# A projection with more rounded parts and one more tap for ScalarE and GpSimd, in a two-layer convolution and MLP trunk

## The reference

```python
u = rmsnorm(h, norm_mix[i])
a = jnp.einsum("bsd,de->bse", u, w_pw1) + b_pw1          # 2048 -> 4096
val, gate = jnp.split(a, 2, axis=-1)
v = val * jax.nn.sigmoid(gate)
v = causal_depthwise_conv(v, w_dw) + b_dw                # 31 taps, per channel
v = rmsnorm(v, g_norm)
v = jax.nn.silu(v)
return jnp.einsum("bsd,de->bse", v, w_pw2) + b_pw2       # "pw2"; then h = h + m
```

## Time and profile before

| | |
|---|---|
| median of 3 runs | 2257.8 us |
| the profiled execution's own time | 2257.75 us |
| its span, first to last instruction | 2256.0 us |
| PE / DVE / ACT / POOL busy | 99% / 63% / 51% / 7% of the span |
| the projection's stage | about 34 us to 215 us |
| mean granted clock of TensorE | 0.999 |

### The profile page before, as it was taken

One profiled execution on the slowest core, in us unless ns is written; L12 is line 12 of the kernel. 1 busy time (PEld: TensorE's weight loads), 2 busy tenths in 40 slices (PEclk: granted clock), 3 DMA queues, 4 the chain that ended last, 5 costly groups with the idle time before them and its releaser, 6 DMA issues.

```text
span 2256.0 us, 29803 instructions
## 1 busy us (share of the span) xinstructions
PE 2236.2 (99%) x10300; PEld 1864.8 (83%) x10300; DVE 1429.1 (63%) x1597; ACT 1145.3 (51%) x1424; POOL 157.1 (7%) x183
## 2 busy tenths in 40 slices
PE   8999999999999999999999999999999999999998
PEld 7998788888888888888888888888888888888886
DVE  6999776555545545566766667665456455556665
ACT  5666555535534534556644444555345345345555
POOL 3888000000000000000000000000000000000000
PEclk9999999999999999999999999999999999999999
DMA  9544477756756856777777677777567567567773
GB/s 340 166 155 145 145 251 256 236 193 206 255 190 196 269 187 204 251 222 256 221 241 220 217 241 213 264 231 253 189 196 267 191 202 252 199 215 224 261 241 112
DMA packets 494098, 494.86 MB, mean 219 GB/s; under 512 B 257936, under 2 KB 296016, under 8 KB 493264
## 3 DMA queue, kind: packets, MB, share of 16 engines
q1 hardware_dynamic: 492192, 491.31, 67.8%
q10 hardware_dynamic: 1696, 1.67, 0.2%
q0 software_dynamic: 144, 1.05, 0.1%
HBM read 460.42 MB, written 33.55 MB: 219 GB/s over the span
## 4 chain that ended last, share of the span: by engine, by line
PE 98%; DMA 1%; DVE 0%; ACTq 0%; issue 0%; ACT 0%; SPq 0%; DVEq 0%
PE acc L430 29%; PE acc L431 29%; PE acc L432 29%; PE acc L492 3%; PE acc L501 2%; PE acc L503 2%; PE acc L502 2%; PE acc L536 1%; PE acc L566 0%; PE acc L565 0%; PE acc L564 0%; DMA emb<-in_cf_b_pw 0%; ACTq L708 0%; DMA staged<-prows 0%; DMA pT<-staged 0%
## 5 line engine op out<-in xcount | busy, mean ns | idle before, releaser
L927 DVE TENSOR_TENSOR wlo<-raw,whi 128x1024 fp32r<-128x1024 f32 x728 | 880.6, 1221 | 590.1 <-ACT whi L586 586.3
L586 ACT ACTIVATE whi<-raw 128x1024 fp32r<-128x1024 f32 x728 | 762.2, 1057 | 774.8 <-PE acc L432 773.8
L430 PE MATMUL acc<-whi,b_hi 128*128 128x512 f32 x1632 | 635.5, 389 | 0.3 <-DVE b_lo L1028 0.3
L432 PE MATMUL acc<-whi,b_lo 128*128 128x512 f32 x1632 | 634.9, 389 | 0.0
L431 PE MATMUL acc<-wlo,b_hi 128*128 128x512 f32 x1632 | 634.9, 389 | 0.0
L430 PE MATMUL acc<-whi,a_hi 128*128 128x512 f32 x1280 | 497.9, 389 | 0.0
L432 PE MATMUL acc<-whi,a_lo 128*128 128x512 f32 x1280 | 497.9, 389 | 0.0
L431 PE MATMUL acc<-wlo,a_hi 128*128 128x512 f32 x1280 | 497.9, 389 | 0.0
L430 PEld LDWEIGHTS acc<-whi,b_hi 128*128 128x128 f32 x1632 | 306.3, 188 | 64.8 <-DVE b_lo L1028 0.7
L432 PEld LDWEIGHTS acc<-whi,b_lo 128*128 128x128 f32 x1632 | 306.3, 188 | 63.8
L431 PEld LDWEIGHTS acc<-wlo,b_hi 128*128 128x128 f32 x1632 | 306.3, 188 | 63.5 <-issue 0.2
(11 more groups left out here) (161 smaller groups left out, 1244.5 us busy)
## 6 DMA issues: line engine op xcount, KB each, us to landing
raw<-in_mlp_w SPq DMA_DIRECT2D x256, 1024.0 KB, 5.5
raw<-in_sc_w_in SPq DMA_DIRECT2D x48, 1024.0 KB, 5.7
raw<-in_cf_w_pw SPq DMA_DIRECT2D x64, 512.0 KB, 8.7
raw<-in_ple_w_gate SPq DMA_DIRECT2D x32, 1024.0 KB, 6.1
staged<-prows SPq DMA_DIRECT2D x240, 128.0 KB, 3.3
pT<-staged SPq DMA_DIRECT2D x56, 512.0 KB, 3.3
raw<-in_cf_w_pw SPq DMA_DIRECT2D x16, 1024.0 KB, 6.8
raw<-in_sc_w_out SPq DMA_DIRECT2D x16, 1024.0 KB, 7.6
```

Source lines behind the costliest of these rows:

```text
L430: nc.tensor.matmul(o, xhi[:, k, s], hi, start=first and c == 0, stop=False)
L432: mm = nc.tensor.matmul(o, xlo[:, k, s], hi, start=False, stop=last and c == 1)
L586: nc.scalar.activation(whi[:, e % SLOTS, :, :], raw[:, e // 2, 2 * (e % 2):2 * (e % 2) + 2, :], ACT.Copy).then_inc(hi_ready, 1)
L927: nc.vector.tensor_tensor(wlo[:, e % SLOTS, :, :], raw[:, e // 2, 2 * (e % 2):2 * (e % 2) + 2, :], whi[:, e % SLOTS, :, :].bitcast(F32), A ...
```

## The change

- `FULL` goes from 5 to 3: from chunk 1 on, 13 of the 16 parts are rounded. The pieces of x are parts 3 to 8 and 9 to 15.
- `POOL_TAPS` goes from 9 to 10: one more product on ScalarE and one more addition on GpSimd, one tap fewer on VectorE. VectorE's places for `front_w_lo` move one tap later with it; that of `glu(n+1)` stays.
- The rounded x (`front_x_hi`) lies where the residual h does. x is fetched a second time into h, in four transfers of SyncE after the last value half, between the first and the second quarter of pw2's weights. VectorE waits for them ahead of pw2's first bias addition.
- `front_w` alone now lies in the place of the embeddings, and the filler `front_end` goes.

```diff
-    FULL = KC - 11
-    X_PARTS = ((FULL, 10), (10, KC))
+    FULL = KC - 13
+    X_PARTS = ((FULL, 9), (9, KC))
     LAST_ORDER = (0, 4, 5, 1, 2, 6, 7, 3)
-    POOL_TAPS = 9
+    POOL_TAPS = 10
...
+        with ExitStack() as before_h:
+            front_x_hi = before_h.enter_context(nc.sbuf_tensor("front_x_hi", [P, KC - FULL, 2 * P], F32R))
         h = sb("h", [P, 2, D])
...
             front_w = before_emb.enter_context(nc.sbuf_tensor("front_w", [P, 2, 2, KC - FULL, P], F32R))
-            front_x_hi = before_emb.enter_context(nc.sbuf_tensor("front_x_hi", [P, KC - FULL, 2 * P], F32R))
         front_x_lo = X[0][0][:, FULL:, :]
         emb = sb("emb", [P, DEPTH, 2, D])
-        sb("front_end", [P, 256])
...
+        x_again = sem("x_again")
...
-            load_unit(pw2, t_in["cf_w_pw2"][0], None)
+            w_pw2 = t_in["cf_w_pw2"][0]
+            load(pw2.b, w_pw2, 0)
+            sp.wait_ge(val_done, CHUNKS)
+            for j in range(BLOCKS):
+                nc.sync.dma_start(h[:, :, j * NB:(j + 1) * NB], xtok(j)).then_inc(x_again, 16)
+            load(pw2.b + 1, w_pw2, NB)
+            with sp.Fori(2, BLOCKS) as j:
+                load(pw2.b + j, w_pw2, j * NB, 0, exchange(Result(pw2, j - 2)))
             load_mlp(0, pw2)
...
                     dve.wait_ge(bias2_early, 16)
+                    dve.wait_ge(x_again, 16 * BLOCKS)
                     b = bias2_first
```

## The result

The changed kernel takes 2273.49 us (median of four runs, 2272.96 to 2274.13) against 2257.78: ratio 1.0068, interval 1.0056 to 1.0081. It is slower by 15.7 us, three times what I forecast and outside my range. The profiled execution takes 2273.25, its span is 2271.5. Executions of the kernel before fall into two groups about 1.6 us apart (2257.4 to 2258.0, and 2259.0 to 2259.5), and those of most other versions spread likewise, so medians of few runs waver by that.

What follows compares the result with a forecast made beforehand. TensorE was taken as the bound before the change, the chain through VectorE, ScalarE and GpSimd after it. +3.9 us for the stage and +1.1 behind the last chunk, added to 2257.75, gave 2262.7 us; range 2256 to 2268.

Steps and rivals of the forecast that it cites:

- What bounds it: First projection: TensorE sets the pace at 12.21 us a chunk; a chain through VectorE, GpSimd and ScalarE is second, about 11.5.
- TensorE's saving: First projection: fewer full and more rounded products save TensorE 0.146 us a half, 0.29 a chunk, giving a pace of 11.92.
- the split sizes: Rounded blocks grow from 1408 to 1664 columns: VectorE's split takes 1.88 us (+0.26), ScalarE's rounding 1.58 (+0.22).
- the head: Start of the projection: VectorE's two splits of x grow by 0.52 us, moving the first gated product from 34.01 to 34.53.
- The chain up to split B: Within a chunk, additions, products and rounding delay VectorE's gate-half weight split (split B) to +9.84 us from the gated product.
- product 9's wait: ScalarE's last tap product waits 0.18 us for a buffer that GpSimd's second single addition frees, starting at +7.83.
- The rival in which it doesn't wait: ScalarE's last tap product finds its buffer free: period 12.25 us, total 2260.2 us; chance 0.18.
- The step that failed: End of a chunk: VectorE's gate-half split starts unhindered at +9.84 us, two taps follow, next gated product at +12.43.
- this rival: GpSimd's sixth addition holds VectorE's gate-half split 0.72 us, 14 times: +10, 2272.8 us; half the chunks, 2267.7; chance 0.17.
- Behind the last chunk: After the projection's last chunk, GpSimd's late join delays ScalarE's copy and the norm, and TensorE's embedding products: +1.1 us.
- The fetch: Second fetch of x: four 512 KB transfers land by about 230 us, 35 us before their first reader; no cost.
- The later stages are untouched: Stages after the projection and embedding products: the change was taken to add no time there.

Runs made afterwards that it cites:

- v1: Changed kernel with ScalarE's rounding for the gate-half weight split moved into its wait for GpSimd's pair addition; 2258.52 us, ratio 1.0001.
- e1: Changed kernel with nine taps again for ScalarE and GpSimd, keeping 13 rounded parts and the second fetch; 2267.39 us, ratio 1.0041.
- e2: Changed kernel with 11 rounded parts again, keeping ten taps and the second fetch of x; 2259.71 us, ratio 1.0004.
- v2: v1 with nine taps (POOL_TAPS = 9); 2257.87 us, ratio 1.0002.
- v5: v2 with 136 already fulfilled waits spread over the rounded halves of TensorE's program; 2256.73 us, ratio 0.9995.
- e3: Changed kernel with 11 rounded parts and nine taps again, leaving only the second fetch and new place of x; 2257.70 us, ratio 0.9999.
- e5: e3 with 120 already fulfilled waits at the start of TensorE's program; 2260.85 us, ratio 1.0013.
- e4: Changed kernel plus one wait: GpSimd's sixth single addition in chunks 0 to 13 starts only after VectorE's gate-half weight split; 2265.41 us, ratio 1.0034.
- v3: v1 plus a wait: GpSimd's fourth single addition starts only after VectorE's gate-half weight split; 2265.95 us, ratio 1.0034.
- v4: v1 with 136 already fulfilled waits at the start of TensorE's program; 2260.33 us, ratio 1.001.

## Why the prediction was wrong

- **What bounds it, TensorE's saving, the split sizes, the head**: right. Blocks took 1.88 and 1.58 us, TensorE's halves in v1 give 11.93 a chunk (11.92 worked out), the first gated product came 0.09 us earlier than forecast.
- **The chain up to split B**: right to 0.02 us, product 9's wait of 0.18 included (the four products and the step to the rounding take 1.81 us, without a wait 1.63). The rival in which it doesn't wait is out.
- **The step that failed** is "split B starts at +9.84 ... L1141 at +12.43". I put GpSimd's sixth addition at +9.86 and let the split through; it began at +9.83, and the split lasts 2.48 us instead of 1.88 in all of the 14 chunks, so that the next gated product comes at +13.03. A call between two engines 0.02 us apart decided 8.4 us, and I gave it 0.17 and half of the price in the range. Such a tie is at least an even chance. That this rival's number, 2272.8, came within a microsecond of the result is in part luck: its hold was priced 1.7 us too high in all, and the 2.2 us of the later stages were in no term.
- What I held against that rival was a misreading. In the earlier trace rows split B met a running addition 0.12 us before its recorded end and was not held. From e1, e2, v2 and the changed kernel, the hold ends 0.13 to 0.14 us before the recorded end of the addition, so that row stood just outside the hold and said nothing of an addition met at its start (one chunk of each trace, the additions of a row taken one by one; the hold is the length above that of an undisturbed split):

| kernel | split arrives behind the addition's start by | ... before its recorded end by | held |
|---|---|---|---|
| before | 0.62 | 0.12 | 0.01 |
| e2 | 0.50 | 0.24 | 0.10 |
| v2 | 0.41 | 0.33 | 0.20 |
| e1 | 0.10 | 0.63 | 0.50 |
| changed | 0.02 | 0.73 | 0.60 |
| v5 | 0.11 | | 0.00, the addition is caught |

- By the rule of the Trainium skill that I cited (SBUF — State Buffer, Who interferes with whom), issue order decides. The traces now agree that either can be the blocked one: GpSimd's L1419 lasts 2.26 us behind the split, and the split is held for up to 0.60 behind L1416. Who issued first was what I could not read, and v5 shows that the recorded starts do not give it to 0.1 us.
- **Behind the last chunk**: right, 1.09 measured for 1.1. TensorE's timeline has the wait for ScalarE's copy that I had put at 1.0:

```profile
238.78 3.70 PE L544 MATMUL acc<-wproj,pT 128*128 128x512 f32 x8 [0.82 <-ACT emb L817]
```

- **The fetch**: right (e3).
- **"The later stages are untouched"**: wrong by 2.2 us. The price was in none of my terms. That the program's length matters is shown by e5; that the time is lost where a code load meets an exchange, by the four places in the changed kernel and by the first of them in the other traces. Why a wait of 0.46 us shifts what follows by 0.75 stays open.
- **A term left out**: TensorE's wait for the split of x, which I had only as longer than the 1.17 us of before, is 2.56 us and is followed by half speed; the last section has the rows. In the changed kernel VectorE's chain hides it. v1 pays for it: its chunk 0 takes 12.65 us instead of my 12.0, which is most of the way from my 213.3 to 214.30.

The measured cost of the failed step and the loss in the later stages close the account: 2262.7 + 8.4 + 2.2 = 2273.3.

## What to carry to other kernels

Where two engines may exclude each other, write down who starts first in steady state; if the gap is smaller than the error of your reading, count the held case as at least even, and look whether moving one instruction by half a microsecond breaks the tie. A wait or a reordering on the engine with slack can be worth more than the work that a change moves: here one moved rounding gave back 15 us. And a time difference of a tenth of a per cent in stages that an edit doesn't touch may be the length of the program; compare offsets stage by stage before explaining it by the edit.

## What the hardware showed that I had not expected

TensorE's granted clock fell after a short wait. Table by stretches of the changed kernel, then of the kernel before, columns as in the earlier trace rows:

```profile
34.00:36.10 2.10, 1.52 (x12) 1.52 (x13) 1.09 (x3) 1.15 (x3) 0.00 (x0) 1.00 1.13 387
36.10:39.50 3.40, 3.40 (x19) 3.40 (x18) 3.40 (x7) 3.40 (x7) 1.06 (x2) 0.51 1.01 421
39.50:50.00 10.50, 10.50 (x79) 10.18 (x79) 9.61 (x19) 6.10 (x12) 8.51 (x10) 1.00 0.73 282
```

```profile
36.10:39.50 3.40, 3.40 (x25) 3.25 (x25) 3.40 (x7) 3.10 (x6) 1.70 (x2) 1.00 1.01 417
```

The mean of 0.51 is its 1.2 GHz level. TensorE's timeline has the idle time that came first, which was 1.17 before:

```profile
34.58 0.39 PE L509 MATMUL acc<-front_x_hi,front_w 128*128 128x256 f32 x1 [2.56 <-DVE a_hi L1159]
```

With 1.17 us of idleness the clock stayed at 2.4 GHz, before the change and in e2, e3 and e5. Behind 2.56 us it fell for 3.4 us in the changed kernel, e1, e4, v1, v3, v4 and v5; in v2, with the same 2.56, it stayed at 1.00:

```profile
34.75 0.39 PE L509 MATMUL acc<-front_x_hi,front_w 128*128 128x256 f32 x1 [2.56 <-DVE a_hi L1159]
...
36.10:39.50 3.40, 3.40 (x30) 3.40 (x30) 3.40 (x7) 3.40 (x6) 0.89 (x2) 1.00 1.02 424
```

In v3 it fell once more, behind the wait of 2.19 us that ends at 230.31; in the changed kernel it did not behind the 0.82 us that end at 238.78. So the idle time alone doesn't settle it; what else does is open. While the lower clock lasts, rounded matmuls start 0.21 us apart instead of 0.12.

A GpSimd addition and a VectorE subtraction, both reading SBUF, hold each other whole, with 0.12 us of grace at an addition's end in the kernel before. A split that arrives within a row of additions goes in behind the one that is running, and the next is caught in its turn (e2: the sixth, 2.13 us long). And 120 more waits at the head of TensorE's program, on a semaphore that the wait ahead of them has already seen, delay its start by 2 us (8.27 instead of 6.31).
